# A first stage reordered around the left half of the tokens, zero products around the first transposes, and an output projection woven into an attention stage

## What is computed

```python
def pool_layer(x, mem, ...):                     # first layer
    proj = rmsnorm(x, norm_mix) @ w_in           # 1024 x 1024: stage "in"
    u_pool, q_mem = proj[..., :768], proj[..., 768:]
    grouped = grouped_product(multiscale_pool(u_pool), w_group) * scale
    mk, mv = split(rmsnorm(mem, mem_norm) @ w_mem_kv)     # stages "mem_a", "mem_b"
    mem_out = memory_attention(q_mem, mk, mv)    # 4 heads, softmax over 256 memory tokens
    x = x + concatenate([grouped, mem_out]) @ w_out       # stage "a_out"
    return x + swiglu(rmsnorm(x, norm_ffn), w_gu, w_down)

def sb_layer(x, mem, k_sh, v_sh, ...):           # second layer
    proj = rmsnorm(x, norm_mix) @ w_q            # stage "q"
    sb_out = stick_breaking_attention(...)       # 12 heads, in 6 pairs
    mem_out = memory_attention(...)              # 4 heads, in 2 pairs: "mem_b"
    x = x + concatenate([sb_out, mem_out]) @ w_out        # stage "b_out"
    return x + swiglu(rmsnorm(x, norm_ffn), w_gu, w_down) # "b_gu", "b_down"
```

## Time and profile before

| | us |
|---|---|
| median of 3 runs | 999.17 |
| lowest and highest | 997.36, 999.43 |
| the profiled execution's own time | 998.59 |
| its span, first to last instruction | 996.8 |
| PE (TensorE matmul) busy | 969.5, 97% of the span |
| PEld (weight load) busy | 779.8 |
| DVE busy | 576.7 |
| ACT busy | 495.0 |

### The profile page before, as it was taken

One profiled execution on the slowest core, in us unless ns is written; L12 is line 12 of the kernel. 1 busy time (PEld: TensorE's weight loads), 2 busy tenths in 40 slices (PEclk: granted clock), 3 DMA queues, 4 the chain that ended last, 5 costly groups with the idle time before them and its releaser, 6 DMA issues.

```text
span 996.8 us, 12359 instructions
## 1 busy us (share of the span) xinstructions
PE 969.5 (97%) x4788; PEld 779.8 (78%) x4788; DVE 576.7 (58%) x851; ACT 495.0 (50%) x686; POOL 5.7 (1%) x13
## 2 busy tenths in 40 slices
PE   6999999999999998999999999999999999999996
PEld 5777888888878875888888888877777788888885
DVE  5654756655356455475665437578874676545434
ACT  5664644434345564454444335556675464435332
POOL 0000000000000000000000001000000000000000
PEclk9999999999999998999999999999999999999998
DMA  9624545555445420454554548533224455545551
GB/s 324 213 86 148 208 172 190 189 174 195 180 169 177 161 85 1 172 209 168 195 184 172 225 174 313 193 132 127 85 96 158 169 172 185 191 170 190 196 184 42
DMA packets 25924, 168.76 MB, mean 169 GB/s; under 512 B 2792, under 2 KB 3798, under 8 KB 6679
## 3 DMA queue, kind: packets, MB, share of 16 engines
q1 hardware_dynamic: 24647, 163.57, 45.9%
q0 software_dynamic: 1232, 4.57, 1.2%
HBM read 167.05 MB, written 1.08 MB: 169 GB/s over the span
## 4 chain that ended last, share of the span: by engine, by line
PE 93%; DVE 3%; ACT 2%; DMA 1%; issue 1%; SPq 0%; ACTq 0%; DVEq 0%
PE ps L1437 79%; PE ps L1553 1%; PE ps L2033 1%; PE ps L1735 1%; PE ps L2044 1%; DMA x_sb<-in_x 1%; PE ps L2063 1%; PE ps L2132 1%; PE ps L1798 1%; PE ps L1627 1%; PE ps L1618 1%; PE ps L1513 1%; PE ps L1590 1%; PE ps L1856 1%; PE ps L1667 1%
## 5 line engine op out<-in xcount | busy, mean ns | idle before, releaser
L871 DVE TENSOR_TENSOR w_both<-raw,w_both 128x2048 fp32r<-128x2048 f32 x150 | 342.0, 2285 | 210.3 <-ACT w_both L409 210.2
L1437 PE MATMUL ps<-w_both,a_hi 128*128 128x512 f32 (+1 forms) x1536 | 416.0, 393 | 3.2 <-DVE m_lo L909 1.9
L409 ACT ACTIVATE w_both<-raw 128x2048 fp32r<-128x2048 f32 x150 | 286.4, 1916 | 188.8 <-DMA raw<-in_down 43.5
L1437 PEld LDWEIGHTS ps<-w_both,a_hi 128*128 128x128 f32 x1536 | 282.2, 189 | 63.7 <-issue 9.3
L1437 PE MATMUL ps<-w_both,a_lo 128*128 128x512 f32 (+1 forms) x768 | 235.6, 388 | 0.0
L1437 PEld LDWEIGHTS ps<-w_both,a_lo 128*128 128x128 f32 x768 | 143.9, 188 | 30.4
L1437 PE MATMUL ps<-w_both,h_hi 128*128 128x512 f32 x576 | 158.3, 396 | 0.0
L1437 PEld LDWEIGHTS ps<-w_both,h_hi 128*128 128x128 f32 x576 | 107.5, 188 | 25.6
L1437 PE MATMUL ps<-w_both,h_lo 128*128 128x512 f32 x288 | 90.5, 395 | 0.0
L1437 PE MATMUL ps<-w_both,m_hi 128*128 128x512 f32 x256 | 72.1, 404 | 2.3 <-ACT projA L490 1.4
L587 ACT ACTIVATE mlp_a<-ps,tiny 128x256 f32<-128x256 f32 x44 | 18.5, 471 | 98.2 <-PE ps L1437 98.2
(11 more groups left out here) (239 smaller groups left out, 686.3 us busy)
## 6 DMA issues: line engine op xcount, KB each, us to landing
raw<-in_a_gu SPq DMA_DIRECT2D x22, 1024.0 KB, 4.8
raw<-in_b_gu SPq DMA_DIRECT2D x22, 1024.0 KB, 4.8
raw<-in_up SPq DMA_DIRECT2D x16, 1024.0 KB, 4.8
raw<-in_down SPq DMA_DIRECT2D x16, 1024.0 KB, 4.8
raw<-in_a_down SPq DMA_DIRECT2D x11, 1024.0 KB, 4.8
raw<-in_b_down SPq DMA_DIRECT2D x11, 1024.0 KB, 4.7
raw<-in_front SPq DMA_DIRECT2D x8, 1024.0 KB, 5.1
raw<-in_gates SPq DMA_DIRECT2D x8, 1024.0 KB, 4.8
```

The lines of the kernel that those rows point to most:

```text
L409: A_(ring(w_hi, us)[:, 0:n], ring(raw, us)[:, 0:n], ACT.Copy).then_inc(s_hi, 1)
L871: V.tensor_tensor(ring(w_lo, us)[:, 0:n], ring(raw, us)[:, 0:n], ring(w_hi, us)[:, 0:n].bitcast(fp32), ALU.subtract).then_inc(s_lo, 1)
L1437: ins = MM(ps[:, b + T, 0:wd], chT(parts[ap_], c, T), wp[wp_][:, off:off + wd], start=(c == first and pn == 0), stop=(c == last and pn == 2))
```

## The change

It has three parts. The loads at the start: the left half of x is first, the right half of x moves behind the second weight unit, one load of "mem_a" moves ahead of `wgrp` and the tables, and `mem` moves behind the third unit. TensorE's start: three products of a zeroed tile `pc` (128 x 128 times 128 x 512, float32) ahead of the first transposes and two behind the transposes of the left half of x; the right half's transposes now stand behind the first two pieces of "in"; the pieces of the last two units are in an order that completes the left result earlier, and ScalarE empties it at `s_half`. The stage of the second layer: six left-column pieces of "b_out" (`out_piece`) stand between the steps of the last stick-breaking pairs and the memory heads; the right-column pieces follow; the splits of the units 2 and 3 of "b_out" move forward on ACT and DVE; the memory heads use other PSUM banks. Zeroed products write bank 7 and are not read.

```diff
         def _(sp):
-            sp.dma_start(ident[:, :], A["ident"]).then_inc(s_cst, 16)
-            sp.dma_start(gamrow[0:NGROW, :], A["gamma_rows"]).then_inc(s_cst, 16)
...
             x_half(0)
+            sp.dma_start(ident[:, :], A["ident"]).then_inc(s_cst, 16)
+            sp.dma_start(gamrow[0:NGROW, :], A["gamma_rows"]).then_inc(s_cst, 16)
             in_half(0, s_inl)
-            x_half(1)
             in_half(1, s_raw[0])
...
             job("in", 1, 2)
+            x_half(1)
+            job("in", 2, 3)
             sp.dma_start(memx...).then_inc(s_mem, 16)
-            job("in", 2, 4)
+            job("in", 3, 4)
             sp.dma_start(poolM[:, :], A["pool"]).then_inc(s_pin, 16)
+            job("mem_a", 0, 1)
             sp.dma_start(wgrp...)
...
+            job("mem_a", 1, 2)
...
@@ ScalarE, start @@
-            act.wait_ge(s_cst, 32)
-            A_(ident_r[:, :], ident[:, :], ACT.Copy).then_inc(s_idr, 1)
...
             transposed_hi(k_x, to_a, (2, 3))
+            split_hi(U0["in"] + 2)
...
             squares("a_mix", x_sb, 1)
             transposed_hi(k_m, to_m, (0,))
-            split_hi(U0["in"] + 2)
-            transposed_hi(k_m, to_m, (1,))
             split_hi(U0["in"] + 3)
-            transposed_hi(k_m, to_m, (2,))
+            transposed_hi(k_m, to_m, (1, 2))
             split_hi(U0["mem_a"])
+            act.wait_ge(s_cst, 32)
+            A_(ident_r[:, :], ident[:, :], ACT.Copy).then_inc(s_idr, 1)
+
+            act.wait_ge(s_half, HALF["in"] + 1)
+            empty_group(G0["in"], both(projA, D, 0), "a_mix")
             transposed_hi(k_m, to_m, (3,))
-            empty_wide("in", projA, 4, "a_mix", U0["mem_a"] + 1)
+            split_hi(U0["mem_a"] + 1)
+            act.wait_ge(s_mm, U0["in"] + 4)
+            empty_group(G0["in"] + 1, both(projA, D, 512), "a_mix")
@@ ScalarE, memory heads of the second layer @@
             sb_hi(4)
+            split_hi(U0["b_out"] + 2)
+            sb_hi(5)
+            mem_copy("mem_b", 0)
             mem_exps("mem_b", 2)
-            mem_copy("mem_b", 0)
-            sb_hi(5)
             mem_exps("mem_b", 3)
             mem_copy("mem_b", 1)
             mem_hi("mem_b", 0)
+            split_hi(U0["b_out"] + 3)
             mem_hi("mem_b", 1)
-            rest("b_out", 4)
@@ VectorE, the same place @@
             mem_norm("mem_b", 0)
+            mem_norm("mem_b", 1)
+            sb_lo(4)
             mem_max("mem_b", 2)
-            mem_norm("mem_b", 1)
             mem_max("mem_b", 3)
-            sb_lo(4)
+            split_lo(U0["b_out"] + 2)
+            sb_lo(5)
+            mem_copy("mem_b", 0)
             mem_norm("mem_b", 2)
-            mem_copy("mem_b", 0)
-            sb_lo(5)
             mem_norm("mem_b", 3)
             mem_copy("mem_b", 1)
             mem_lo("mem_b", 0)
+            split_lo(U0["b_out"] + 3)
             mem_lo("mem_b", 1)
-            rest("b_out", 4)
@@ TensorE, start @@
+            def warm_up(n):
+
+                for _k in range(n):
+                    MM(bank(7), pc[:, 0:P], pc[:, :], start=True, stop=True)
+            pe.wait_ge(s_dve, 3)
+            warm_up(3)
             pe.wait_ge(s_cst, 32)
             nc.tensor.transpose(bank(0, 0, NGROW), gamrow[0:NGROW, :], ident[0:NGROW, 0:NGROW]).then_inc(s_gamT, 1)
-            for nb in range(2):
-                pe.wait_ge((s_xl, s_x)[nb], 16)
-                flips(lambda T: tok(x_sb, D, T), (2 * nb, 2 * nb + 1))
+            pe.wait_ge(s_xl, 16)
+            flips(lambda T: tok(x_sb, D, T), (0, 1))
+            warm_up(2)
             pe.wait_ge(s_gam, 1)
...
+            for n in range(4):
+                pe.wait_ge(*((s_lo, 1) if n == 3 else (s_ino, n + 1)))
+                ins = in_piece(0, n // 2, n % 2)
+                if n == 3:
+                    ins.then_inc(s_mm, 1)
+                if n == 1:
+                    pe.wait_ge(s_x, 16)
+                    flips(lambda T: tok(x_sb, D, T), (2, 3))
+            pe.wait_ge(s_lo, 2)
+            in_piece(1, 0, 0)
+            in_piece(1, 0, 1)
+            in_piece(1, 1, 0)
+            mem_flip(0)
+            in_piece(1, 1, 1).then_inc(s_mm, 1)
+            pe.wait_ge(s_lo, 3)
+            in_piece(2, 0, 0)
+            in_piece(2, 0, 1)
+            mem_flip(1)
+            in_piece(2, 1, 0)
+            pe.wait_ge(s_lo, 4)
+            in_piece(3, 0, 0)
+            mem_flip(2)
+            in_piece(3, 0, 1).then_inc(s_half, 1)
+            in_piece(2, 1, 1).then_inc(s_mm, 1)
+            mem_flip(3)
+            in_piece(3, 1, 0)
+            in_piece(3, 1, 1).then_inc(s_mm, 1)
             block_job("mem_a", 1, MH, need=normed("mem"))
@@ TensorE, memory heads of the second layer @@
+            def out_piece(c):
+
+                if c == 0:
+                    group_free(G0["b_out"])
+                    pe.wait_ge(s_wt, 5)
+                if c % 2 == 0:
+                    pe.wait_ge(s_lo, U0["b_out"] + c // 2 + 1)
+                pe.wait_ge(s_olo, O0["sb"] + c + 1)
+                out_columns(c // 2, 0, (c % 2,))
+            for p in range(5):
...
+            pe.wait_ge(s_wt, 4)
+            mem_logits("mem_b", 0, qTB[:, 6 * S:8 * S], mkTB)
+            sb_sums(5)
+            out_piece(0)
+            sb_values(4)
+            out_piece(1)
             sb_values(5)
-            pe.wait_ge(s_wt, 6)
             mem_logits("mem_b", 1, qTB[:, 6 * S:8 * S], mkTB)
+            out_piece(2)
             mem_transposes("mem_b", 0)
+            out_piece(3)
             mem_values("mem_b", 1, 0)
+            out_piece(4)
             mem_transposes("mem_b", 1)
+            out_piece(5)
             mem_values("mem_b", 1, 1)
+            group_free(G0["b_out"] + 1)
+            pe.wait_ge(s_olo, O0["mem_b"])
+            for j in range(3):
+                out_columns(j, 1).then_inc(s_mm, 1)
+            pe.wait_ge(s_lo, U0["b_out"] + 4)
             pe.wait_ge(s_olo, O0["nsa"])
-            wide_job("b_out", 4, MH, tail=x_flips("b_out", 0))
+            out_columns(3, 0).then_inc(s_half, 1)
+            out_columns(3, 1, (0,))
+            x_flips("b_out", 0)()
+            out_columns(3, 1, (1,)).then_inc(s_mm, 1)
```

More of the change, by code:

```diff
@@ L65 @@
 SET = {n: i for i, n in enumerate(["a_mix", "mem", "a_ffn", "b_mix", "b_ffn", "mix2", "branches", "mlp2"])}
-HALF = {n: i for i, n in enumerate(["a_out", "a_down", "q", "b_out", "b_down", "branch_a", "out2", "down2"])}
+HALF = {n: i for i, n in enumerate(["in", "a_out", "a_down", "q", "b_out", "b_down", "branch_a", "out2", "down2"])}
 A0 = {"mem_a": 0, "mem_b": 4, "nsa": 8, "dsa": 24}
@@ L342, in _ @@
             sp.dma_start(onehot[0:33, :], A["onehot"]).then_inc(s_tin, 16)
-            for name in ("mem_a", "mem_b", "a_out"):
+            job("mem_a", 1, 2)
+            for name in ("mem_b", "a_out"):
                 job(name)
@@ L452, in mem_exps @@
                 for T in range(2):
-                    ins = A_(mem_probs(stage, h, S * T, S * T + S), bank(MEM_L[stage][h // 2] + h % 2, S * T, S * T + S), ACT.Exp,
+                    ins = A_(mem_probs(stage, h, S * T, S * T + S), bank(MEM_L[h // 2] + h % 2, S * T, S * T + S), ACT.Exp,
                              bias=m_max[h][:, T:T + 1], accum_out=m_sum[h][:, T:T + 1])
@@ L459, in mem_copy @@
                 act.wait_ge(s_pt, A0[stage] + 2 * p + 1)
-                A_(mem_probsT(2 * p), bank(MEM_T[stage][p]), ACT.Copy).then_inc(s_ptc, 1)
+                A_(mem_probsT(2 * p), bank(MEM_L[p]), ACT.Copy).then_inc(s_ptc, 1)
             def mem_hi(stage, p):
@@ L967, in mem_copy @@
                 dve.wait_ge(s_pt, A0[stage] + 2 * p + 2)
[L968 removed]
+                V.tensor_copy(mem_probsT(2 * p + 1), bank(MEM_L[p] + 1)).then_inc(s_ptd, 1)
             def mem_lo(stage, p):
@@ L1571, in _ @@
+            flips(lambda T: tok(x_sb, D, T), (0, 1))
+            warm_up(2)
             pe.wait_ge(s_gam, 1)
             def mem_flip(r):
[L1574 to L1580, removed]
+                pe.wait_ge(s_mem, 16)
+                pe.wait_ge(s_nlo, 4 * SET["a_mix"] + r + 1)
+                flips(lambda T: tok(memx, D, T), (r,))
@@ new lines, in _, with in_piece @@
+            in_need = normed("a_mix")
+            def in_piece(j, nb, k):
+                return mult_pieces(U0["in"] + j, [(2 * j + k, 2 * PAIR[G0["in"] + nb], 512, D * k + 512 * nb)], AH, 0, KC - 1,
+                                   need=in_need)
+            for n in range(4):
[6 more added lines that the diff above has]
+                    flips(lambda T: tok(x_sb, D, T), (2, 3))
@@ L1644, in mem_transposes @@
                 if p:
-                    pe.wait_ge(s_e, A0[stage] + 4 if stage == "mem_a" else A0[stage] + 2)
+                    pe.wait_ge(s_e, A0[stage] + 4)
                 for e in range(2):
@@ L1652, in mem_transposes @@
                             lo = S * T + P * M
-                            ins = nc.tensor.transpose(bank(MEM_T[stage][p] + e, o, o + P), mem_probs(stage, h, lo, lo + P),
```

(12 more changed lines are left out.)

17 lines of the change are left out of this document (4 added, 13 removed).

## The result

The changed kernel takes 989.07 us (median of 5; 988.66 to 989.43) against 999.17 (996.92 to 999.82). The ratio is 0.9912, 95% interval 0.9895 to 0.9929: faster by 0.9%, 10.1 us in the medians. The forecast was 988.9, the range 985.5 to 993.5. The profiled execution takes 988.66 us with a span of 986.9.

The account below looks back on a forecast made before the run. TensorE was taken to bound the kernel, leaving its idle and low-clock time to win. 3.3 us (start) + 7.0 (attention stage) = 10.3: profiled 998.59 becomes 988.3, from the median 988.9; range 985.5 to 993.5.

Parts of the forecast that it names:

- The start: From the first loads to "mem_a", which was to begin at 35.3 instead of 38.67: 3.3 us won, between 2.0 and 4.2.
- a wait for the right half of x: Start, after two pieces end at 12.6 us: TensorE waits until 13.5, between 12.7 and 14.7; called the step that decides.
- the 21.8 of the sum: Start, TensorE's work after that load: 8 transposes, 14 pieces, 16 transposes of `mem`, 0.87 + 19.2 + 1.75 us.
- the zeroed products: Start: needed only to have the clock high by 13.5 us; no gain of their own was given.
- The attention stage: Second layer, last sums to end of "b_out": 29.4 us work, 1.8 us waits; 7.0 us won, between 4.0 and 8.3.
- the price of a piece: Six matmuls of "b_out" or "in" cost 1.37 us, a quarter of 5.48; 16 pieces of "b_out" 21.9 us.
- The waits: Attention stage: 1.1 us for DVE's copy behind the split, 0.7 us at the end from the late "b_gu" load.
- The clock: Attention stage and "b_out": the 90 matmuls lost 1.7 us to the low clock; the sum assumed a high clock.
- A: Rival, start: the right half of x lands at about 16.5 us, start wins only 0.3 us, 991.9 us; 15%.
- B: Rival, start: zeroed products do not raise the clock, or it falls before the right half; about 990.9 us; 15%.
- C: Rival, attention stage: softmax chain keeps TensorE waiting longer, clock falls again, stage wins 3.5, 992.4 us; 15%.
- D: Rival, attention stage: nothing overlaps, pieces and splits stand in series with the softmax, kernel slower at 1002.6 us; 3%.

Follow-up runs that it names:

- e9: The changed kernel with the right half of x issued ahead of the second unit of "in": 989.86 us.
- e3: The changed kernel without the five zeroed products: 989.88 us.
- e4: The changed kernel with the three zeroed products ahead of the transposes, without the two behind them: 990.5 us.
- e11: The changed kernel, but ScalarE empties the left result of "in" only when all four units are multiplied, as before: 990.81 us.
- e10: The changed kernel with all loads at the start in the order of the kernel before: 990.38 us.
- e7: The edit of e6, with VectorE's split of the third "b_out" unit also moved behind the memory heads' copy and normalizations: 987.61 us.
- e6: The changed kernel with two right-column pieces of "b_out" in the places of the fifth and sixth left-column piece: 988.28 us.
- e5: The changed kernel again, nothing edited, as the reference of its group: 989.08 us.
- e8: The kernel before with nine zeroed products in the idle stretches of the attention stage, nothing else moved: 995.3 us.
- e12: The kernel before, unchanged, profiled once more: one execution, 1000.43 us.
- e1: The kernel before with only the start's part of the change, attention stage as before: 994.04 us, ratio 0.996.

## Why the prediction was right, point by point

**The start** was put at 3.3 us and gave 3.7 (3.4 over the four traces). The steps held: the first piece at 9.05 us (about 9.9 forecast), a wait for the right half of x until 12.83 (13.5 forecast, range 12.7 to 14.7), then no wait at all. The 0.8 us at the first piece brought nothing, since the wait takes it up. The load landed 0.7 us earlier than forecast, and the work behind it took 22.1 us, 0.3 more than the 21.8 of the sum, mostly since the eight transposes behind the wait take 1.09 us and not 0.87; 0.4 us are left. Two things in its reasoning were weaker than they sounded. The wait for the right half "decides" only as long as the second unit comes in time: e9 takes it away and loses 0.6 us. And the zeroed products were treated as a condition with no price; e3 gives it, 0.8 us for all five. The last two added nothing in e4's trace, but its other five executions speak for more. The statement of the Trainium skill, "TensorE: Matmul & The Clock Gate", Part 1, that the ramp is under 1% of a typical kernel, agrees with the size, 0.8 of 989 us.

The experiments split the start: emptying early 1.3 us (e11), the order of loads 1.3 (e10), zeroed products 0.8 (e3). Their sum is 3.4, as much as the whole gain, but each is taken from one trace, with the other parts in place, and such readings differ by 0.6 us among the four traces of the changed start. No run takes the new place of the right half's transposes away by itself, so what that is worth is not shown; a sum that comes out does not make it nothing, since the parts can depend on each other.

**The attention stage** was put at 7.0 us and gave 5.8. Two terms of this step were mis-sized. The first is an error of adding: 29.4 us of work and 1.8 us of waits make 31.2, and I took 0.5 off for slack between two waits that lie 18 us apart; both came (0.75 and 0.78 us idle, 1.53 together). What is left, 31.92 - 1.53 = 30.4 us, is work, 1.0 us more than the sum had.

The second term, and the larger error, is the price of a piece. It is 1.37 to 1.40 us behind other pieces or behind transposes; behind the value products, whose weights have 64 columns, it is 1.58 or 1.59, and so it is behind the logits (e7's trace: 379.29, 1.59 us). Four of the pieces stand in such a place, 0.84 us more; the eight transposes of x, which follow a wait, take 1.09 us where the sum had 0.87. That accounts for the 1.0 us. With the 0.5 of the slack, and waits that are 0.3 shorter than forecast, it makes the 1.2 us by which the stage missed.

What differs in the rows is the weight load of such a piece. Behind the value products the weight path does nothing for 0.39 us before it; behind transposes the load follows without a gap:

```profile
384.74 0.76 PEld L1438 LDWEIGHTS ps<-w_both,m_hi 128*128 128x128 f32 x4 [0.39 <-issue]
...
387.00 0.76 PEld L1438 LDWEIGHTS ps<-w_both,m_hi 128*128 128x128 f32 x4
```

No run tests why the load comes later there. The trace of the kernel before had this price, for instance behind the logits of the first layer, and I had not looked at it:

```profile
63.12 1.93 PE ps L1637 x16
65.04 1.58 PE ps L1437 x6
```

So the stretch of 31.9 us lies outside the 27 to 31 us that the prediction named as what the profile would show.

**The waits** that I named were the ones that came: DVE's split ahead of the copy (1.1 us forecast, 0.75 idle), the late load of "b_gu" (0.7 and 0.78). e6 removes the second and e7 the first: the stretch goes from 31.83 us (e5) to 31.08 and then to 30.30, and the medians fall by 0.8 and 0.7 us. Each cause is shown.

**The clock** carried more than the text gave it. The text names its loss in the 90 matmuls, 1.7 us; the sum, which has all work at full speed, contains without a word the slow value products and transposes of two rows more (1.97 and 1.66 us). e8 puts the whole at 3.0 us of the stage's 5.8. With it goes the spread of the executions: 6.2 us in the group of e8 for the kernel before, 1.4 for e8, and 0.8 over the first five executions of the changed kernel. So the gain is 10.1 us against the median of before, and only some 6 against its best executions; in the group of e9 to e12, where more of them were of this kind, the median of before was 995.3.

**The total** is closer than its terms, and that is luck. The stage gave 1.2 us less than forecast. The start gave 0.4 more, 0.3 more came between "mem_a" and the last sums, which the sum did not have, and 0.1 behind the stage: 9.9 us in the span instead of 10.3. The forecast of the median came within 0.2 us since this median lies 0.41 us above the profiled execution, where the forecast carried over the 0.58 of before.

**The rivals.** A (the right half at about 16.5 us) did not occur: the latest landing with this order of loads was 14.64 us, in e1, within the 12.7 to 14.7 of the forecast. B and C did not occur in a trace of the changed kernel; D, the slower one, needed 10.3 us of added waits in the stage, and there are 1.5.

## What to carry to other kernels

When an in-order engine waits for a chain through other engines, put independent work between the steps, but price each piece by what stands ahead of it, and keep long instructions of the helping engines behind the chain's own steps (e7). An idle stretch costs twice where the clock falls: its own length, and the slow work behind it. So fill it even with work that nobody reads if nothing else is there (e8: 3.0 us of the stretch, 3.7 in the medians, nothing against the best executions of before). When one load is brought forward, ask which one becomes the last to arrive, and count the steps behind it: here a load that still has to be split twice had to come before one that is used directly (e9: 0.6 us).

## What was not expected of the hardware

Products of zeroed memory raise the clock and hold it (e8): three of them, started at 1.62 us, take 4.37 us (4.32 to 5.47 in the other traces), and the transposes behind them 1.04 instead of 1.97 us. The clock column of the profile reads 1.00 in the first microseconds although the transposes and the first matmuls of before took about twice as long there as later:

```profile
10.00:14.00 4.00, 3.90 (x13) 3.42 (x14) 1.81 (x4) 1.23 (x3) 0.00 (x0) 1.00 1.01 420
```

At the start the durations must be read, not the column. The clock did not fall over 2.1 us without work in e4's trace, and fell in the kernel before around 384 us, in e12 after windows with 1.09 and 0.43 us of work in two us each. And the same order of loads brought the right half of x at anything from 12.83 to 14.64 us.
